# Sixteen more tokens taken out of the dense expert projection of a hybrid block, and the last gate unit in two halves

## The chip, the cores and the metric

One Trainium2 chip, one NeuronCore of it. The metric is the device time of one execution in microseconds; of the kernel before there are three runs. All data is float32; the matmuls of the large projections are float32 products made of three fp32r matmuls.

## What is computed

One layer of a trunk over 512 tokens of width 1024: a parallel mix of windowed attention and retention, then a product-key expert mixer (PEER), a gated per-layer embedding, and a final norm. The part that is changed is the expert mixer, and at the end the gate:

```python
q = (h @ w_query).reshape(B, S, PEER_HEADS, 2, half)
s1, s2 = scores of q[..., 0, :] and q[..., 1, :] with 128 sub keys each
v1, i1 = top_k(s1, 16);  v2, i2 = top_k(s2, 16)
top_s, top_pos = top_k(v1[:, None] + v2[None, :], 16)      # 16 of 256 pairs, for each of 8 heads
expert_idx = i1 * 128 + i2 of these pairs;  gates = softmax(top_s)
u = expert_down[expert_idx]                                # 128 rows of 1024 for each token
act = gelu(einsum('td,ted->te', h, u))
y = einsum('te,ted->td', act * gates, expert_up[expert_idx])
x = x + y
x = x + sigmoid(rms_norm(x) @ w_ple_gate) * (p @ w_ple_proj)
return rms_norm(x)
```

There are 128 x 128 = 16384 experts, each one row of `expert_down` and one of `expert_up`.

## The kernel before

**Stages.** Activations are kept transposed, model width on the partitions and tokens on the columns. Every weight comes as a unit of 128 x 1024 (0.5 MB); `UNITS` (line 44 on) lists all 390 in the order of their use. SP loads a unit into one of 4 `raw` slots (line 437) as soon as `lo_done` says that POOL has finished with that slot. ScalarE writes its upper part `w_hi` (line 496), POOL its lower part `w_lo` (line 450), into rings of 8, and PE multiplies in three matmuls (`mm3`, lines 848 to 850).

The expert mixer handles 384 of the 512 tokens densely, and the last 128 sparsely. For the 384 dense tokens PE computes the inner products with all 16384 rows of `peer_down`: 128 units (`down`, line 1061), each 24 matmuls of 384 columns, 8 units to a turn, 16 turns. ScalarE takes the GELU of each result (line 701) and writes pairs of units to memory (line 704). In turns 9 to 14 PE also makes the gates of all experts of a token from one-hot vectors: DVE compares the keys with an iota (`compare`, line 1531) and multiplies one of the two one-hots with the gate (`times_gate`, line 1538), for four tokens at a time, 16 such quads `q` in a turn `j`; PE multiplies them (`scatter`, line 1081) and ScalarE stages the result and writes it out (lines 707 to 719). DVE's `compare` may be four quads ahead of PE. Before that, PE transposes the selected keys and gates, after `SELECT_AT` = 3 units of turn 8 (lines 1102 to 1110). In the up projection (`up`, line 1121) DVE multiplies activations by gates (`weigh`, line 1578), ScalarE and DVE split the result (lines 771, 1595), and PE multiplies it with the 128 units of `peer_up`, 18 matmuls of 512 columns each. `weigh` reads gates and activations back from memory, in pieces issued by ScalarE (`read_back`, line 725).

**The sparse tokens** have one token on each partition. For each of 128 rows (8 heads x 16), POOL fetches 128 rows of `peer_down` by an indirect DMA into one of four slots (`u_ring`, line 470), and DVE multiplies them with the tokens' activations `h_tok` and adds up (`dot`, line 1196). `h_tok` is made once, by 16 matmuls (line 1050). Later the rows of `peer_up` are fetched and added likewise (`axpy`, line 1567).

**What sets the order.** There is no scheduler: each engine's program is written out by hand, with waits on semaphores. POOL's queue holds the lower parts unit by unit; at which unit a fetch stands in it is given by `EARLY_FETCH` and `fetch_down_at` (lines 151 to 161), for dots that DVE makes between the steps of its top-k (`together`, `best`, `decode`; 66 of them), 4 behind the exponential's argument, 6 behind the gates (`DOTS_EXP`, `DOTS_SELECT`), and then between one-hots (`DOT_QUADS`, line 1149). A fetch also waits for the dot that used its slot four rows before (line 469). ScalarE gives the upper part of unit e + 5 just before the GELU of unit e (`gelu`, line 688). At the end of the last down turn (lines 784 to 796) it also splits the first two experts' weights, and it reads back the first two pieces after the third unit.

**The end.** For each of 8 units of the gate (`pg`, line 1164) PE makes 24 matmuls of 512 columns; DVE scales, ScalarE takes the sigmoid, DVE multiplies and adds, ScalarE squares; `add_up(3)` sums the squares over partitions, and the final norm follows (lines 1625 to 1639).

## Time and profile before

| | us |
|---|---|
| three runs | 2020.37, 2021.49, 2022.61; median 2021.49 |
| profiled execution, its own time | 2022.7 |
| its span in the trace | 2020.9 |
| PE busy | 1994.2 (99%) |
| PE weight loads busy | 1760.5 (87%) |
| DVE busy | 1372.2 (68%) |
| ScalarE busy | 803.7 (40%) |
| POOL busy | 1197.5 (59%) |
| mean DMA rate | 225 GB/s |

Busy times are sums over instructions of one execution; the engines work side by side, so they do not add up to the span. Matmuls overlap, and their ends are modelled: what one costs is read from the distance between the starts, not from its duration. "Released by" names the instruction that ended a wait last.

### The profile page before, as it was taken

How to read it: one execution, taken by the hardware profiler on the slowest of the kernel's cores; microseconds unless marked ns; L12 is line 12 of the kernel's file. 1: busy time of each engine (PE TensorE's matmuls, PEld its weight loads, DVE VectorE, ACT ScalarE, POOL GpSimd, SP SyncE). 2: the span in 40 equal slices, each digit the busy share in tenths (PEclk: the TensorE clock that was granted, in tenths of full speed). 3: DMA queues.
4: the chain of work that ended last, by engine and by line, in shares of the span. 5: the costliest groups of instructions: out<-in, count | busy, mean ns of one | idle time of the engine just before them, and what ended most of it. 6: DMA issues, size and time to landing. Idle time of an engine off the chain costs nothing.

```text
span 2020.9 us, 28806 instructions
## 1 busy us (share of the span) xinstructions
PE 1994.2 (99%) x10155; PEld 1760.5 (87%) x10155; DVE 1372.2 (68%) x2241; ACT 803.7 (40%) x1075; POOL 1197.5 (59%) x650
## 2 busy tenths in 40 slices
PE   7999999999999999999999999999999999999997
PEld 6888888887888888999999999999888888888886
DVE  6424242333722399899997878782797899888946
ACT  5222222233643343333334666665443333333352
POOL 5342424243245244878888555555899888888821
PEclk9999999999999999999999999999999999999998
DMA  6232323133233322889999788888999999999911
GB/s 215 73 114 61 117 62 108 66 120 94 74 94 105 114 84 86 307 294 318 324 319 323 288 302 298 301 303 296 341 384 382 372 364 353 359 369 367 349 62 42
DMA packets 167334, 455.00 MB, mean 225 GB/s; under 512 B 13264, under 2 KB 62416, under 8 KB 165456
## 3 DMA queue, kind: packets, MB, share of 16 engines
q1 hardware_dynamic: 58032, 209.04, 30.8%
q0 software_dynamic: 36864, 134.23, 17.3%
q10 hardware_dynamic: 72352, 110.64, 16.0%
q8 instruction: 47, 0.77, 0.2%
q14 instruction: 39, 0.32, 0.0%
HBM read 396.71 MB, written 54.53 MB: 223 GB/s over the span
## 4 chain that ended last, share of the span: by engine, by line
PE 95%; DVE 2%; ACT 1%; DMA 1%; ACTq 0%; issue 0%; SPq 0%; DVEq 0%
PE bank L848 29%; PE bank L850 29%; PE bank L849 29%; PE bank L1089 4%; PE bank L955 1%; PE bank L1038 1%; PE bank L1023 1%; PE bank L999 0%; PE bank L1009 0%; DVE bank L1244 0%; DMA xT<-x_cols 0%; ACTq L731 0%; PE bank L924 0%; DVE h_lo L1252 0%; PE bank L912 0%
## 5 line engine op out<-in xcount | busy, mean ns | idle before, releaser
L450 POOL TENSOR_TENSOR w_lo<-raw,w_hi 128x1024 fp32r<-128x1024 f32 x390 | 937.6, 2412 | 709.7 <-ACT w_hi L496 706.3
L848 PE MATMUL bank<-h_hi,w_hi 128*128 128x384 f32 (+1 forms) x1552 | 560.0, 361 | 0.4 <-ACT scr L701 0.4
L850 PE MATMUL bank<-h_hi,w_lo 128*128 128x384 f32 (+1 forms) x1552 | 548.5, 353 | 0.0
L849 PE MATMUL bank<-h_lo,w_hi 128*128 128x384 f32 (+1 forms) x1552 | 548.3, 353 | 0.0
L496 ACT ACTIVATE w_hi<-raw 128x1024 fp32r<-128x1024 f32 x390 | 407.5, 1057 | 172.5 <-PE bank L850 62.6
L850 PEld LDWEIGHTS bank<-h_hi,w_lo 128*128 128x128 f32 x1552 | 291.9, 188 | 21.2
L848 PEld LDWEIGHTS bank<-h_hi,w_hi 128*128 128x128 f32 x1552 | 292.2, 188 | 20.6 <-issue 0.6
L849 PEld LDWEIGHTS bank<-h_lo,w_hi 128*128 128x128 f32 x1552 | 292.2, 188 | 20.1
L850 PE MATMUL bank<-w_hi,b_lo 128*128 128x512 f32 x768 | 298.8, 389 | 0.0
L849 PE MATMUL bank<-w_lo,b_hi 128*128 128x512 f32 x768 | 298.8, 389 | 0.0
L848 PE MATMUL bank<-w_hi,b_hi 128*128 128x512 f32 x768 | 298.8, 389 | 0.0
L1595 DVE TENSOR_TENSOR b_lo<-scr,b_hi 128x384 fp32r<-128x384 f32 x128 | 210.3, 1643 | 71.9 <-ACT b_hi L771 71.9
L1204 DVE SCALAR_TENSOR_TENSOR xT<-xT,bank 128x1024 f32<-128x1024 f32 x128 | 154.9, 1212 | 28.5 <-DMA xT<-peer_down,scr 27.9
L850 PEld LDWEIGHTS bank<-w_hi,b_lo 128*128 128x128 f32 x768 | 144.1, 188 | 30.0
L849 PEld LDWEIGHTS bank<-w_lo,b_hi 128*128 128x128 f32 x768 | 144.1, 188 | 29.9
L848 PEld LDWEIGHTS bank<-w_hi,b_hi 128*128 128x128 f32 x768 | 144.1, 188 | 29.9
L771 ACT ACTIVATE b_hi<-scr 128x384 fp32r<-128x384 f32 x128 | 67.2, 525 | 255.5 <-PE bank L850 129.2
L480 POOL DMA_INDIRECT scr<-peer_up,scr x128 | 137.6, 1075 | 51.6 <-DVE bank L1575 31.7
L1575 DVE SCALAR_TENSOR_TENSOR bank<-scr,bank 128x1024 f32<-128x1024 f32 x127 | 162.2, 1277 | 0.8
L713 ACT ACTIVATE scr<-bank 128x512 f32<-128x512 f32 x96 | 109.3, 1138 | 107.3 <-PE bank L1089 107.3
L470 POOL DMA_INDIRECT xT<-peer_down,scr x128 | 122.1, 954 | 31.0 <-issue 16.5
L701 ACT ACTIVATE scr<-bank 128x384 f32<-128x384 f32 x128 | 62.9, 492 | 176.7 <-PE bank L850 173.0
(185 smaller groups left out, 2545.0 us busy)
## 6 DMA issues: line engine op xcount, KB each, us to landing
raw<-weights SPq DMA_DIRECT2D x390, 512.0 KB, 4.6
act_scratch<-scr ACTq DMA_DIRECT2D x64, 384.0 KB, 4.8
gate_scratch<-scr ACTq DMA_DIRECT2D x12, 2048.0 KB, 8.0
scr<-gate_scratch ACTq DMA_DIRECT2D x22, 768.0 KB, 7.7
scr<-act_scratch ACTq DMA_DIRECT2D x22, 768.0 KB, 12.6
xT<-gate_scratch ACTq DMA_DIRECT2D x10, 768.0 KB, 7.5
xT<-act_scratch ACTq DMA_DIRECT2D x10, 768.0 KB, 12.1
scr<-scr ACTq DMA_DIRECT2D x20, 128.0 KB, 2.7
```

Of the source, the lines that this page charges most:

```text
L450: return nc.gpsimd.tensor_tensor(w_lo[:, s, :], raw[:, s % RAW, :], w_hi[:, s, :].bitcast(F32), ALU.subtract)
L470: pool.indirect_dma_start(u_ring[:, n % U_SLOTS, :], None, down_d, bass.IndirectOffsetOnAxis(ap=expert_of[:, n:n + 1], axis=0)).then_inc(u ...
L480: pool.indirect_dma_start(v_slot(n), None, up_d, bass.IndirectOffsetOnAxis(ap=expert_of[:, n:n + 1], axis=0)).then_inc(v_landed[n % V_SLOT ...
L496: nc.scalar.activation(w_hi[:, u_mod, :], raw[:, s, :], ACT.Copy).then_inc(hi_done, 1)
L713: nc.scalar.activation(stage[:, b, :, t:t + 4].rearrange("p j t -> p t j"), scattered(q), ACT.Copy).then_inc(stage_ready, 1)
L848: nc.tensor.matmul(out, a_hi, c_hi, start=first, stop=False)
L849: nc.tensor.matmul(out, a_hi, c_lo, start=False, stop=False)
L850: return nc.tensor.matmul(out, a_lo, c_hi, start=False, stop=last)
L1089: ins = nc.tensor.matmul(scattered(q)[:, x, :], onehot(q, x, 0).bitcast(F32), gated[q % 4][:, x, :], start=True, stop=True)
L1204: stt(out=row, in0=row, scalar=1.0, in1=h_tok, op0=ALU.mult, op1=ALU.mult, accum_out=dots[:, n:n + 1]).then_inc(dot_done, 1)
L1575: ins = stt(out=y_sparse, in0=v_slot(n), scalar=a, in1=y_sparse, op0=ALU.mult, op1=ALU.add)
L1595: tt(b_lo[:, c % 4, 0:TD], wgt[:, c % 2, :], b_hi[:, c % 4, 0:TD].bitcast(F32), ALU.subtract).then_inc(wgt_split, 1)
```

## The change

`TZ` = 368 instead of 384 tokens go through the dense down projection; the 16 tokens 368 to 383 (`NX`) take its result from fetched rows. For them the partitions are laid out as 8 groups of 16 tokens: `copies_hi` and `copies_lo` hold each token's activations 8 times (written by ScalarE), so that one fetch brings the rows of one of the 16 picks for all 8 heads of all 16 tokens, and 16 fetches bring them all. The expert numbers are computed from the transposed keys and turned onto the partitions by DVE (`turn`), and the 16 results are turned back, go through the GELU, and are multiplied into the transposed gates of these tokens; the activations in memory are 1.0 there (a memset). `h_tok` is rewritten for the copies (`REP_AT`) and again for the sparse tokens (`TOK_AT`). There are thus 144 fetches and dots instead of 128.

The order is rewritten with it: the exponential is taken after 3 units of turn 8 (`EXP_AT`) instead of at its start, the selection after 6 instead of 3. DVE makes 74 dots ahead of the one-hots instead of 76, 6 in a row behind the third quad, 10 in each of the last three scatter turns instead of 8, and the last 15 (`NLAST`) behind the last one-hot, ahead of `weigh`. All 144 fetches have units of their own in POOL's queue (`FETCH_AT`), the last at the unit 130 from the first down unit, that is the third of `peer_up`. The scatter turns 0 to 2 are written out instead of looped.

The last gate unit is made in two halves of 256 tokens, in two banks, and everything behind it up to the squares' sum as well.

```diff
+HALVES = (slice(0, S // 2), slice(S // 2, S))
 TD = S - P
 TDT = TD // P
+NX = 16
+TZ = TD - NX
 TG = 32
...
-SELECT_AT = 3
+EXP_AT, SELECT_AT = 3, 6
...
-DOTS_EXP, DOTS_SELECT, DOTS_START = 4, 6, 4
+DOTS_EXP, DOTS_SELECT = 4, 4
 DOTS_EARLY = (PH - 1) * DOTS_DECODE + (PH - PLAIN_HEADS) * DOTS_HEAD + DOTS_EXP + DOTS_SELECT
-DOT_QUADS = tuple(range(1, TG // 2, 2))
+ODD = tuple(range(1, TG // 2, 2))
+DOT_QUADS = ((2, 2, 2, 2, 2, 2, 7, 9, 11, 13, 15), ODD, (1, 3, 5, 11, 13, 15)) + 3 * (tuple(sorted(ODD + (4, 10))),)
+NMAIN = DOTS_EARLY + DOT_QUADS[0].count(2)
+NROWS = NPAIR + NX
+REP_AT, TOK_AT = (0, 1), (2, 4)
+NGATE = sum(map(len, DOT_QUADS))
+NLAST = NROWS - DOTS_EARLY - NGATE
 AXPY_LAG = 8
-EARLY_FETCH = (8, 8, 9, 9, 11, 11, 13, 14, 14, 15, 15, 16, 17, 17, 20, 21, 21, 22, 23, 24, 25, 27, 28, 29, 30, 30,
-               31, 31, 32, 33, 33, 36, 36, 37, 37, 38, 40, 40, 42, 43, 45, 45, 46, 46, 47, 47, 49, 49, 51, 51, 52,
-               52, 53, 55, 55, 57, 57, 58, 58, 59, 60, 60, 61, 63, 63, 64, 65, 65, 67, 67, 69, 69, 70, 70, 71, 72,
-               72, 73, 73, 74, 74, 75, 76, 77)
-
-
-def fetch_down_at(n):
-
-    if n < len(EARLY_FETCH):
-        return DN0 + EARLY_FETCH[n]
-    return DN0 + STEP * FIRST_Z + 10 + n - DOTS_EARLY - DOTS_START
+EARLY_FETCH = (8, 8, 9, 9, 11, 11, 14, 15, 15, 16, 16, 17, 18, 18, 21, 22, 22, 23, 24, 25, 26, 28, 29, 30, 31,
+               31, 32, 32, 33, 34, 34, 37, 37, 38, 38, 40, 42, 42, 44, 45, 47, 47, 48, 48, 49, 49, 51, 51, 53, 53,
+               54, 54, 55, 57, 57, 59, 59, 60, 60, 61, 62, 62, 63, 66, 66, 67, 68, 68, 70, 70, 72, 72, 73, 73)
+FETCH_AT = EARLY_FETCH + (74, 74, 75, 75, 76, 76)
+FETCH_AT += tuple(STEP * (FIRST_Z + 1 + j) + q // 2 + 3 for j in range(len(DOT_QUADS)) for q in DOT_QUADS[j])[6:]
+FETCH_AT += tuple(NKEY - STEP + 3 + 8 * i // NLAST for i in range(NLAST))
+assert len(EARLY_FETCH) == DOTS_EARLY and len(FETCH_AT) == NROWS
+assert all(x <= y for x, y in zip(FETCH_AT, FETCH_AT[1:])) and FETCH_AT[-1] < NKEY + LEAD
...
 FETCH_DOWN, FETCH_UP, ADD_UP_AT = {}, {}, {}
+for _s, _u in enumerate(FETCH_AT):
+    FETCH_DOWN.setdefault(DN0 + _u, []).append(_s)
 for _n in range(NPAIR):
-    FETCH_DOWN.setdefault(fetch_down_at(_n), []).append(_n)
...
+        def last_gate(x):
+
+            return bank[:, 5 - 3 * x, HALVES[x]]
...
+                for r in FETCH_DOWN.get(u, ()):
+                    extra, n = row_of(r)
+                    if r == 0:
...
+                    if extra:
+                        pool.wait_ge(extra_ready, 1)
+                    elif n % TOPK == 0:
                         pool.wait_ge(expert_ready, n // TOPK + 1)
...
-                nc.scalar.activation(act[:, c % 4, :], bank[:, c % 2, 0:TD], ACT.Gelu_apprx_tanh).then_inc(act_ready, 1)
+                nc.scalar.activation(act[:, c % 4, 0:TZ], bank[:, c % 2, 0:TZ], ACT.Gelu_apprx_tanh).then_inc(act_ready, 1)
...
-                if c == 0:
+                if c < 2:
+                    copies, h = ((copies_hi, h_hi), (copies_lo, h_lo))[c]
+                    nc.scalar.activation(copies.rearrange("p k (g t) -> p k g t", t=NX),
+                                         h[:, :, TZ:TD].unsqueeze(2).to_broadcast([P, KT, P // NX, NX]),
+                                         ACT.Copy).then_inc(copies_ready, 1)
+                if c == EXP_AT:
                     sc.wait_ge(top_ready, 1)
                     nc.scalar.activation(gate_s.rearrange("p t n -> p (t n)"), gate_s.rearrange("p t n -> p (t n)"),
                                          ACT.Exp).then_inc(gexp_ready, 1)
@@ -755,7 +792,11 @@
                 gelu(FIRST_Z, c)
...
+            for j in range(1, TOK_AT[0] + 1):
+                gate_turn(j)
+            sc.wait_ge(extra_dotted, 1)
+            nc.scalar.activation(act_extra, dots_extra, ACT.Gelu_apprx_tanh).then_inc(extra_gelu, 1)
+            with sc.Fori(TOK_AT[0] + 1, NTG // 2) as j:
                 gate_turn(j)
...
-            sc.wait_ge(dot_done, NPAIR)
+            sc.wait_ge(dot_done, NROWS)
...
-                    pe.wait_ge(sq_ready, KT * (r + 1))
                     for t in range(TT):
+                        if t % 2 == 0:
+                            pe.wait_ge(sq_ready, KT * (r + 1) + t // 2)
                         ins = nc.tensor.matmul(bank[:, 7, t:t + 1], sq[:, (KT - 1) % 2, P * t:P * t + P],
                                                ones[:, 0:1], start=False, stop=t == TT - 1)
...
+            def token_rows(of):
+
+                for k in range(KT):
+                    for n, h in enumerate((h_hi, h_lo)):
+                        ins = nc.tensor.matmul(h_tok[:, P * k:P * k + P], of(h, k), ident_r[:, :],
+                                               start=n == 0, stop=n == 1)
+                ins.then_inc(htok_done, 1)
...
-                    ins = mm3(bank[:, c % 2, 0:TD], w_hi[:, s, P * k:P * k + P], w_lo[:, s, P * k:P * k + P],
-                              h_hi[:, k, 0:TD], h_lo[:, k, 0:TD], k == 0, k == KT - 1)
+                    ins = mm3(bank[:, c % 2, 0:TZ], w_hi[:, s, P * k:P * k + P], w_lo[:, s, P * k:P * k + P],
+                              h_hi[:, k, 0:TZ], h_lo[:, k, 0:TZ], k == 0, k == KT - 1)
...
                 for c in range(STEP):
                     down(j + (FIRST_Z + 1), c, halfway=lambda: scatter(j, 2 * c))
                     scatter(j, 2 * c + 1)
+                    if isinstance(j, int) and (j, c) == REP_AT:
+                        pe.wait_ge(dot_done, NMAIN)
+                        pe.wait_ge(copies_ready, 2)
+                        token_rows(lambda h, k: (copies_hi if h is h_hi else copies_lo)[:, k, :])
+                    if isinstance(j, int) and (j, c) == TOK_AT:
+                        pe.wait_ge(dot_done, NMAIN + NX)
+                        token_rows(lambda h, k: h[:, k, TD:S])
...
-            scatter_turn(0)
-            with pe.Fori(1, NTG // 2) as j:
+            for j in range(TOK_AT[0] + 1):
+                scatter_turn(j)
+            with pe.Fori(TOK_AT[0] + 1, NTG // 2) as j:
                 scatter_turn(j)
...
+            last = UNIT[("pg", KT - 1)]
+            pe.wait_ge(lo_done, last + 1)
+            for x in range(2):
+                pe.wait_ge(pg_free, KT - 4 + x)
+                for k in range(KT):
+                    ins = mm3(last_gate(x), w_hi[:, last % RING, P * k:P * k + P], w_lo[:, last % RING, P * k:P * k + P],
+                              h_hi[:, k, HALVES[x]], h_lo[:, k, HALVES[x]], k == 0, k == KT - 1)
+                ins.then_inc(proj_done, 1)
             add_up(3)
...
+            nc.vector.memset(act[:, :, TZ:TD], 1.0).then_inc(filled, 1)
...
+            step(stt(out=ids_extra, in0=keysT[:, 0, TZ:TD], scalar=float(NKEY), in1=keysT[:, 1, TZ:TD],
+                     op0=ALU.mult, op1=ALU.add))
+            turn(ids_extra)
+            mark(tt(expert_extra, turned[:, 0, :], turned[:, 1, :], ALU.add), extra_ready)
...
                     times_gate(j, q)
-                    if j == 0 and q == 2:
-                        next_dots(DOTS_START)
-                    if q in DOT_QUADS:
-                        dot()
-
+                    next_dots(DOT_QUADS[j].count(q))
+                    if done[0] == NMAIN + NX and not extras[0]:
+                        extras[0] = 1
+                        ve.wait_ge(dot_done, NMAIN + NX)
+                        turn(dots_extra)
+                        mark(tt(dots_extra, turned[:, 0, :], turned[:, 1, :], ALU.add), extra_dotted)
+
+            extras = [0]
             compare(0, 0)
             for j in range(NTG // 2):
+                if j == NTG // 2 - 2:
+                    ve.wait_ge(extra_gelu, 1)
+                    step(tt(bank[:, 6, TZ:TD], bank[:, 6, TZ:TD], act_extra, ALU.mult))
                 one_hots(j)
             ve.wait_ge(oh_used, TD // 4)
             for k in range(2):
                 ve.wait_ge(p_hi_ready, k + 1)
                 mark(tt(b_lo[:, 4 + k, :], pT[:, k, :], b_hi[:, 6 + k, :].bitcast(F32), ALU.subtract), p_split)
+            next_dots(NLAST)
...
+            m = KT - 1
+            z = tile2[:, tiles[0] % 2, :]
+            ve.wait_ge(pproj_ready, KT)
+            for x, a in enumerate(HALVES):
+                ve.wait_ge(proj_done, OUT[("pg", m)] + 1 + x)
+                mark(tt(z[:, a], last_gate(x), rrms[:, a], ALU.mult), scaled_ready)
+                if x == 0:
+                    add_square(3, m - 1)
+                ve.wait_ge(tile_ready, tiles[0] + 1 + x)
+                step(tt(prod[:, a], z[:, a], pproj[m][:, a], ALU.mult))
+                mark(tt(xT[:, m, a], xT[:, m, a], prod[:, a], ALU.add), x_ready)
```

## Rows read from the trace of the kernel before

**Rows 1.** The page, part 4: the chain that ended last, its shares by engine.
```profile
PE 95%; DVE 2%; ACT 1%; DMA 1%; ACTq 0%; issue 0%; SPq 0%; DVEq 0%
```

**Rows 2.** Windows: stretch, length, busy PE, PEld, DVE, ACT, POOL, clock, DMA share, GB/s.
```profile
800.00:1066.00 266.00, 266.00 (x1537) 266.00 (x1536) 248.18 (x619) 98.12 (x130) 221.11 (x135) 1.00 0.88 305
...
1100.00:1388.00 288.00, 288.00 (x1933) 288.00 (x1932) 226.94 (x289) 174.54 (x193) 165.59 (x98) 1.00 0.80 294
1388.00:1420.00 32.00, 31.64 (x183) 31.35 (x183) 4.83 (x7) 13.35 (x19) 17.11 (x9) 1.00 0.96 328
```

**Rows 3.** Timeline of PE, three widths: first, last of 59, 36, 37 steps.
```profile
899.70 0.33 PE L848 MATMUL bank<-h_hi,w_hi 128*128 128x384 f32 x1
...
909.93 0.33 PE L850 MATMUL bank<-h_hi,w_lo 128*128 128x384 f32 x1
...
1995.73 0.39 PE L850 MATMUL bank<-h_hi,w_lo 128*128 128x512 f32 x1
...
2003.89 0.39 PE L850 MATMUL bank<-h_hi,w_lo 128*128 128x512 f32 x1
...
404.77 0.28 PE L848 MATMUL bank<-w_hi,h_hi 128*128 128x256 f32 x1
...
409.21 0.28 PE L849 MATMUL bank<-w_lo,h_hi 128*128 128x256 f32 x1
```

**Rows 4.** The chain in order of time: the token rows; columns start, us, what.
```profile
726.16 1.73 PE bank L1052 x16
```

**Rows 5.** Timeline of DVE from the gates to the 80th dot.
```profile
1078.26 0.23 DVE L1520 COPY scr<-scr 128x128 f32<-128x128 f32 x1
...
1085.61 1.22 DVE L1204 SCALAR_TENSOR_TENSOR xT<-xT,bank 128x1024 f32<-128x1024 f32 x1
...
1093.99 2.35 DVE L1535 TENSOR_TENSOR b_hi<-bank,scr 128x1024 fp32r<-128x1024 f32 x2
...
1096.85 1.22 DVE L1535 TENSOR_TENSOR b_lo<-bank,scr 128x1024 fp32r<-128x1024 f32 x1
...
1106.15 1.22 DVE L1204 SCALAR_TENSOR_TENSOR xT<-xT,bank 128x1024 f32<-128x1024 f32 x1 [1.19 <-DMA xT<-peer_down,scr]
```

**Rows 6.** Timeline of PE: last selection transposes, first scatter.
```profile
1079.45 0.27 PE L1109 MATMUL bank<-small,scr 128*128 128x128 f32 x1
...
1102.44 1.05 PE L1089 MATMUL bank<-scr,b_hi 128*128 128x128 f32 x8
```

**Rows 7.** Timeline of POOL: lowered weights and fetches in its queue.
```profile
1088.62 2.40 POOL L450 TENSOR_TENSOR w_lo<-raw,w_hi 128x1024 fp32r<-128x1024 f32 x1
...
1093.40 2.41 POOL L450 TENSOR_TENSOR w_lo<-raw,w_hi 128x1024 fp32r<-128x1024 f32 x1
...
1100.59 0.94 POOL L470 DMA_INDIRECT xT<-peer_down,scr  x1 [3.66 <-DVE xT L1204]
```

**Rows 8.** The fetches of peer_down rows, from issue to landing.
```profile
DMA to landing us min/median/max: 4.6/6.3/10.6
```

**Rows 9.** Timelines of POOL and of ACT in the last down turn.
```profile
1390.65 4.75 POOL L450 TENSOR_TENSOR w_lo<-raw,w_hi 128x1024 fp32r<-128x1024 f32 x2 [2.56 <-ACT w_hi L496]
...
1400.99 5.08 ACTq L731 DMA_DIRECT2D scr<-act_scratch  x1
1406.19 1.06 ACT L496 ACTIVATE w_hi<-raw 128x1024 fp32r<-128x1024 f32 x1 [6.57 <-issue]
```

**Rows 10.** The chain around the start of the up projection.
```profile
1420.49 0.23 PE bank L848
```

**Rows 11.** Windows: a pause of PE, the up stage; columns as in rows 2.
```profile
495.00:505.00 10.00, 7.98 (x33) 6.09 (x32) 9.19 (x15) 4.41 (x16) 2.34 (x1) 0.83 0.27 80
...
1430.00:1445.00 15.00, 15.00 (x68) 12.43 (x67) 13.78 (x9) 4.72 (x6) 14.28 (x9) 1.00 1.02 372
```

**Rows 12.** The chain behind the last unit.
```profile
2005.90 0.70 DVE scr L1634
...
2008.02 1.88 PE bank L904 x8
```

More of the change, by code:

```diff
@@ L212, in block_program @@
         sub_keys = small[:, 424:680].rearrange("p (a k) -> p a k", a=2)
+        same_half = small[:, 680:712].rearrange("p (a k) -> p a k", a=2)
         misc = sb("misc", [P, 128])
@@ L460, in _ @@
                 lower(u % RING).then_inc(lo_done, 1)
-                for n in FETCH_DOWN.get(u, ()):
-                    if n == 0:
+                for r in FETCH_DOWN.get(u, ()):
+                    extra, n = row_of(r)
+                    if r == 0:
                         pool.wait_ge(x_spilled, 16)
@@ L709, in stage_gates @@
                 b, t = q // (TG // 4), 4 * (q % (TG // 4))
-                if t == 0 and not isinstance(j, int):
+                if t == 0 and not (isinstance(j, int) and j == 0):
                     sc.wait_ge(gate_written[b], 16 * j)
@@ L737, in gate_turn @@
                     stage_gates(j, 2 * c + 1)
-                    if c == 1 and not isinstance(j, int):
+                    if c == 1 and not (isinstance(j, int) and j == 0):
                         store_gates(j - 1, 1)
@@ L757, in _ @@
             sc.dma_start(pT[:, :, :], pT_d).then_inc(p_landed, 16)
-            with sc.Fori(1, NTG // 2) as j:
+            for j in range(1, TOK_AT[0] + 1):
[3 more added lines that the diff above has]
+            with sc.Fori(TOK_AT[0] + 1, NTG // 2) as j:
                 gate_turn(j)
@@ L833, in _ @@
             root(2)
-            for m in range(KT):
+            for m in range(KT - 1):
                 run_ahead(UNIT[("pg", m)] + 4)
@@ L1049, in _ @@
                     pe.wait_ge(ident_ready, 1)
-                    for k in range(KT):
-                        for n, h in enumerate((h_hi, h_lo)):
-                            ins = nc.tensor.matmul(h_tok[:, P * k:P * k + P], h[:, k, TD:S], ident_r[:, :],
-                                                   start=n == 0, stop=n == 1)
-                    ins.then_inc(htok_done, 1)
+                    token_rows(lambda h, k: h[:, k, TD:S])
                 if m == 0:
@@ L1163, in _ @@
                 embed(m)
-            for m in range(KT):
+            for m in range(KT - 1):
                 columns(("pg", m), h_hi, h_lo, tiles=(u_ready, 2 * KT) if m == 0 else None,
@@ L1168, in _ @@
                     spread(2)
+            last = UNIT[("pg", KT - 1)]
+            pe.wait_ge(lo_done, last + 1)
+            for x in range(2):
+                pe.wait_ge(pg_free, KT - 4 + x)
[3 more added lines that the diff above has]
+                ins.then_inc(proj_done, 1)
             add_up(3)
@@ L1196, in dot, with turn @@
             def dot():
-                n = done[0]
+                r = done[0]
                 done[0] += 1
-                if n == 0:
-                    ve.wait_ge(htok_done, 1)
-                ve.wait_ge(u_landed[n % U_SLOTS], 16 * (n // U_SLOTS + 1))
-                row = u_ring[:, n % U_SLOTS, :]
+                extra, n = row_of(r)
+                if r in (0, NMAIN, NMAIN + NX):
+                    ve.wait_ge(htok_done, 1 + (r >= NMAIN) + (r >= NMAIN + NX))
+                ve.wait_ge(u_landed[r % U_SLOTS], 16 * (r // U_SLOTS + 1))
+                row = u_ring[:, r % U_SLOTS, :]
+                to = dots_extra if extra else dots
                 stt(out=row, in0=row, scalar=1.0, in1=h_tok, op0=ALU.mult, op1=ALU.mult,
-                    accum_out=dots[:, n:n + 1]).then_inc(dot_done, 1)
+                    accum_out=to[:, n:n + 1]).then_inc(dot_done, 1)
+            def turn(src):
+                step(tt(two_halves, src.unsqueeze(1).to_broadcast([P, 2, NX]), same_half, ALU.mult))
+                step(nc.vector.transpose(turned.rearrange("p a k -> p (a k)"), two_halves.rearrange("p a k -> p (a k)")))
             def together(instructions, more=False):
@@ L1624, in _ @@
             norm_scale(2)
-            for m in range(KT):
+            for m in range(KT - 1):
                 key = ("pg", m)
```

37 lines of the change are left out of this document (29 added, 8 removed).

## The prediction

> **What bounds the kernel now.** I read the chain of waits first: 95% of it is TensorE [rows 1]. The windows by stage say the same: from 800 to 1388 us, in which the dense down projection runs, TensorE is busy in every microsecond, and the granted clock is 1.00 [rows 2]. Only in the last down turn (1388 to 1420 us, eight groups) does it lose 0.36 us, and there the DMA engines are busy for 0.96 of the time although nothing is fetched for the sparse tokens. So a column that leaves the down matmuls is time gained, as long as nobody who feeds TensorE was just in time. The same table warns of this: DVE is busy for 248 of 266 us up to 1066. What it does there does not get shorter by the change.
>
> **Narrower matmuls.** The starts of matmuls of one width give their cost: 59 steps of 384 columns in 10.23 us are 173.4 ns, 36 steps of 512 in 8.16 us are 226.7 ns, 37 steps of 256 in 4.44 us are 120.0 ns [rows 3]. Both differences give 0.417 ns a column. 16 columns less are 6.67 ns, and there are 128 x 24 = 3072 such matmuls: **-20.5 us**. One group of 24 goes from 4.16 to 4.00 us.
>
> The Trainium skill (TensorE: Matmul & The Clock Gate, Back-to-back issue gap) speaks against this: in a stream of weight load and matmul it gives some 81 ns for 128 columns and 131 ns for 512, as an estimate 0.13 ns a column, by which the gain would be 6.4 us. The rows disagree; the measured slope is three times that.
>
> **Work added to TensorE.** The token rows are formed three times instead of once. Once is 16 matmuls in 1.73 us [rows 4], all on the path, so **+3.5 us**. The selection transposes and the one-hot products stay as they are.
>
> **First handover: top-k and one-hots to the scatter.** TensorE now reaches the same point earlier: it begins the down groups at 799.8, so the 71st begins at 799.8 + 70 x 4.00 = 1079.8, where it now makes the selection transposes (they ended at 1079.7 before, after 67 groups). The gates are ready at 1078.3 as before [rows 5], since DVE's work up to there is the same and its fetches are moved to about the same times. So the selection itself waits for nothing. But then only two and a half groups lie before the first scatter instead of five and a half: it is asked for at 1079.8 + 1.2 (nine transposes) + 8.0 + 2.0 = 1091.0, where before it was 1102.4 [rows 6]. DVE: the 74th dot ended at 1086.8 and is fetched at the same time now; with two dots less behind it, but the ids of the extra tokens (four small steps, some 1.7 us together, an estimate by the 0.23 us copy at 1078.26 with as much again for the wait behind each), the first compare is at about 1088.8 against 1093.99. Two compares and one product (1093.99 to 1096.85, 1.14 + 1.14 + 0.6) put the first one-hot at 1091.7: 0.7 us late.
>
> Three one-hots later DVE takes six dots in a row (one and four before), from 1095.1. POOL can issue the last two of these fetches only when the first two dots have freed their slots, at 1096.4 and 1097.7. In the trace the same wait is to be seen: a fetch held up until 1100.6 whose dot came at 1106.15 [rows 5, 7]. With the median 6.3 us from issue to landing [rows 8] the sixth dot ends at 1105.3, and the fourth one-hot is there at 1107.1. TensorE asks for it after 0.7 us of waiting and three steps of 2.9 us (half a group, and 0.9 for a scatter's eight matmuls, whose row shows 1.05 with the last one's end) at 1100.5: 6.3 us late. Together **+7 us**. Bounds: 2 us, if the fetches land after the 4.6 us minimum and the small steps cost nothing, and 11, with the 10.6 us maximum.
>
> From there on DVE has room: 16 x (1.14 + 0.6) + 10 x 1.23 = 40 us of work for a turn of 46.4. The other queues: the two copies of ScalarE, at some 1.06 us each, lie in its 2 us waits for TensorE; if those were gone they would delay the weights by 2 us, with five groups in hand. The memset and the second half of the gates' waits cost nothing beside them. The wait of ScalarE for the extra dots lies after a turn in which they are long done, and the wait of TensorE for the 96th dot comes four one-hots after it. SP's queue only gets its waits answered earlier.
>
> **Second handover: the last dots to the up projection.** Fifteen dots now follow the last one-hot, and DVE weighs the first experts only after them. Their fetches lie in POOL's queue, two behind each lowered weight, over units 123 to 130. A unit with two fetches takes POOL 4.78 us (1088.62 to 1093.40) [rows 7], a group takes TensorE 4.00. POOL begins unit 125 at 1390.7 [rows 9] and would be at 128 at 1405.0, but ScalarE is held for 5.08 us in issuing the read-back of the activations and gives the upper part of that unit at 1406.19 to 1407.25 [rows 9]. That it is held is due to what is in flight, so it is taken as it was. From 1407.3: two units with two fetches (9.6), one lowering (2.4) and the issue, so the last fetch goes out at 1419.5. Landing 6.3, dot 1.3, weighing, its upper and its lower part 2.2: the first expert's weights are ready at 1429.3. Before, TensorE began with them at 1420.49 without a wait [rows 10]. It would now begin at 1420.5 - 8 x 0.16 = 1419.2. So **+10.1 us**. Bounds: 5, with fast landings and the read-back issued without being held, and 19 (the third rival). Behind DVE's dots stand the weighing, then ScalarE's weight upper parts, the last GELU and the next weights' upper parts, which have five units in hand.
>
> **The clock.** Both stalls are longer than any idle time of TensorE in this stage, so it may fall from 2.4 to 1.2 GHz. Where TensorE paused for 2 us near 500 us the mean clock of 10 us was 0.83, 1.7 us of full clock lost [rows 11]. Between nothing and that for each stall I take 1.2 twice: **+2.4 us**.
>
> **The last unit in halves.** 48 matmuls of 256 columns are 5.76 us against 24 x 0.2267 = 5.44: +0.3. Behind them five elementwise steps have half their width: of 0.70 us for 512 columns [rows 12] at most half can go, and each keeps a start of its own, so I take 0.26, -1.3 us in all. Of the eight closing matmuls (1.88 us) [rows 12] half can go ahead: -0.9. **-1.8 us**, between 0 and -2.5.
>
> Sum: -20.5 + 3.5 + 7.0 + 10.1 + 2.4 - 1.8 = +0.7 us. The profiled execution took 2022.7 us, 1.8 more than its span and 1.2 more than the median; set against the median of 2021.5 the forecast is **2022.2 us**, no change that a measurement could tell (0.2%, 4 us).
>
> **Rivals.**
> *The covers hold.* Were neither handover late, 7.0 + 10.1 + 2.4 = 19.5 us go from the forecast and 2002.7 is left. If one of them holds, it is 2011 to 2014. For it: both terms hang on landings, and the spread of these (4.6 to 10.6 us) [rows 8] is as long as the lateness. Against it: three groups of slack are taken from the first handover, and POOL's 37 us (8 x 2.4 + 15 x 1.2) of lowering and fetching in a last turn of 32 us, make TensorE late without any late landing. 0.14 for both, 0.20 for one.
> *No time per column here.* Between 128 columns (1.73 us / 16 = 108 ns) and 256 (120 ns) the spacing hardly follows the width; were this so at 368, the gain would be 3072 x 1.5 ns = 4.5 us. TensorE would come 2.3 us early to the first handover, which had 2.5 in hand, and the second would cost 9: -4.5 + 3.5 + 9 + 1.2 - 1.8 = +7.4, 2029 us. It decides if the next spacing is over 171 ns. Against it: two equal slopes in rows 3. 0.03.
> *The last down turn becomes bound by transfers: slower.* 1388 to 1420 moved 328 GB/s x 32 us = 10.5 MB. 13 fetches of 0.52 MB come on top: 17.3 MB, at the 372 GB/s of 1430 to 1445 [rows 11] 46.5 us. The last fetch lands at 1434.5 and TensorE begins at 1438: 8.7 us more, 2031 us. It decides as soon as the last landing takes more than some 10 us, or the read-back is held for over 9. For it: that stretch's share of 0.96 [rows 2] without any fetch. Against it: the weights run several units ahead, and a busy share does not say that no more could be moved. 0.21. The Trainium skill (Perfetto Trace Analysis, Roofline) puts a single core's ceiling at some 435 GB/s; by that estimate the stretch would take 39.8 us, and no stage of this trace holds such a rate.
>
> **How the numbers follow.** Forecast, both handovers late as worked out: 0.42; its own range is 2017 to 2028 by the bounds of both. Faster by over 4 us: the first rival's 0.34, and 0.03 from the lower end of the forecast. Slower by over 4 us: 0.03 + 0.21 + 0.04 from its upper end, 0.28. Same: 0.35. The range leaves out the full success and the worst of the transfers: 2008 to 2032.
>
> **What would show it.** The down matmuls at 166.7 ns; TensorE waiting 5 to 8 us for DVE at its fourth scatter near 1100 us, the dot before it waiting for a DMA; at the start of the up projection 8 to 12 us of waiting for DVE's lower part, with the last dot of L1204's line just ahead and POOL without a gap; granted clock below 1 behind both; the last PE pieces followed by shorter DVE pieces. The forecast is wrong if TensorE's busy time over its span stays at 99% and the down stage is 17 us shorter, or if ScalarE's issue of the first read-back holds TensorE much longer than the 0.36 us of now.

## The result: 2059.5 us, 1.9% slower

The changed kernel took 2059.5 us (median of four runs, 2052.6 to 2069.7), the kernel before beside it 2020.9 (2020.3 to 2022.6): ratio 1.019, 95% interval 1.017 to 1.022. The forecast was 2022.2, the range 2008 to 2032. The runs of the changed kernel also differ by 17 us, those of the kernel before by 2. The profiled execution has a span of 2061.7 us, 40.8 more than before; all lines below are from profiled executions, one of each kernel.

**The profile after.** The chain that ended last, by engine, and from part 5 of the page the groups of the dot products and of their fetches (busy, mean ns, idle before and what ended it):

```profile
PE 72%; DVE 12%; DMA 7%; POOL 4%; issue 3%; ACT 2%; ACTq 1%; DVEq 0%; SPq 0%; POOLq 0%
...
L1276 DVE SCALAR_TENSOR_TENSOR xT<-xT,bank 128x1024 f32<-128x1024 f32 x144 | 174.2, 1213 | 117.4 <-DMA xT<-peer_down,scr 114.2
...
L501 POOL DMA_INDIRECT xT<-peer_down,scr x144 | 137.1, 952 | 68.7 <-DVE xT L1276 42.6
```

TensorE's share of the chain fell from 95% [rows 1] to 72%. VectorE now waits 114 us for expert rows; before it was 28. The windows, with the columns of [rows 2], show where TensorE stands:

```profile
1050.00:1100.00 50.00, 42.21 (x243) 41.64 (x241) 41.80 (x76) 20.23 (x27) 37.71 (x25) 0.90 0.86 290
1100.00:1150.00 50.00, 38.50 (x228) 38.17 (x228) 38.01 (x50) 18.17 (x21) 20.93 (x13) 0.83 0.49 160
...
1122.00:1132.00 10.00, 9.84 (x42) 9.84 (x43) 5.29 (x7) 1.08 (x1) 0.00 (x0) 0.52 0.30 106
...
1165.00:1415.00 250.00, 241.10 (x1641) 238.39 (x1640) 192.85 (x256) 147.42 (x167) 142.01 (x89) 0.99 0.82 301
...
1400.00:1450.00 50.00, 39.82 (x236) 39.54 (x235) 20.00 (x32) 18.26 (x24) 31.92 (x24) 0.90 1.04 387
```

There are two places with idle TensorE and a granted clock below 1 (1050 to 1150, 1400 to 1470), and a thin loss of 8.9 us in 250 between them. TensorE's timeline has 13 gaps over 0.25 us in this stage, 44.9 us together. These are the first matmuls behind six of them (start, length, line, and in brackets the idle time and its releaser):

```profile
1082.72 0.65 PE L897 MATMUL bank<-h_hi,w_hi 128*128 128x368 f32 x1 [7.79 <-ACT scr L732]
...
1107.54 1.86 PE L1143 MATMUL bank<-scr,b_hi 128*128 128x128 f32 x7 [7.51 <-DVE scr L1625]
...
1122.16 2.07 PE L1143 MATMUL bank<-scr,b_lo 128*128 128x128 f32 x8 [3.98 <-DVE scr L1625]
...
1167.45 0.82 PE L1143 MATMUL bank<-scr,b_hi 128*128 128x128 f32 x5 [1.19 <-DVE scr L1625]
...
1440.55 0.65 PE L897 MATMUL bank<-h_hi,w_hi 128*128 128x368 f32 x1 [10.18 <-ACT scr L732]
...
1461.62 0.77 PE L897 MATMUL bank<-w_hi,b_hi 128*128 128x512 f32 x1 [6.49 <-DVE b_lo L1684]
```

The 7.79 us: the gelu that should have freed a bank stands on ScalarE behind the exponentials, and these wait for VectorE's search. Then come the first scatter, the fourth, the first and the ninth scatter of the turns `j` = 1, 3, 4 and 5, that is the head of each half turn (eight gaps between 0.27 and 2.10, as the one shown; 8.9 in all), a gelu behind the read-back in the last down turn, and the start of the up projection.

**Where VectorE is late.** In the search (800 to 1080 us) the same small steps take longer than before. First the changed kernel, then the kernel before; columns: busy us, mean ns:

```profile
L1577 DVE TENSOR_TENSOR scr<-scr 128x256 f32<-128x256 f32 x16 | 20.0, 1307 | 0.6
...
L1563 DVE SCALAR_TENSOR_TENSOR scr<-scr 128x16 uint32<-128x16 f32 x8 | 17.8, 2219 | 0.3
...
L1556 DVE CAST scr<-scr 128x128 f32<-128x128 uint32 x8 | 3.9, 486 | 0.3
```
```profile
L1499 DVE TENSOR_TENSOR scr<-scr 128x256 f32<-128x256 f32 x16 | 16.7, 1103 | 0.6
...
L1485 DVE SCALAR_TENSOR_TENSOR scr<-scr 128x16 uint32<-128x16 f32 x8 | 14.0, 1746 | 0.3
...
L1478 DVE CAST scr<-scr 128x128 f32<-128x128 uint32 x8 | 1.8, 227 | 0.3
```

A step on 16 elements takes 2.2 us on average, and 0.17 at the least. The timelines of VectorE and of GpSimd (POOL) in the changed kernel say why. Three pairs, each a VectorE row and then the GpSimd row beside it; the first row merges three candidate additions, of 0.41, 7.98 and 0.41 us:

```profile
1044.89 8.65 DVE L1577 TENSOR_TENSOR scr<-scr 128x256 f32<-128x256 f32 x3
...
1045.80 7.12 POOL L477 TENSOR_TENSOR w_lo<-raw,w_hi 128x1024 fp32r<-128x1024 f32 x3
...
955.96 3.79 DVE L1563 SCALAR_TENSOR_TENSOR scr<-scr 128x16 uint32<-128x16 f32 x1
...
954.95 4.75 POOL L477 TENSOR_TENSOR w_lo<-raw,w_hi 128x1024 fp32r<-128x1024 f32 x2
...
1101.48 3.02 DVE L1605 TENSOR_TENSOR scr<-scr 128x16 uint32<-128x16 f32 x1
...
1102.12 2.35 POOL L477 TENSOR_TENSOR w_lo<-raw,w_hi 128x1024 fp32r<-128x1024 f32 x1
```

The small step of the other two pairs ends 0.05 and 0.03 us after the lowering (GpSimd's instruction that makes `w_lo`) does, once after two lowerings in a row (954.95 + 4.75 = 959.70 against 959.75). Of the eight steps of line 1563 the six long ones all end 0.04 to 0.05 us after a lowering; the two of 0.17 us met none. The addition of 7.98 us ended 0.29 us behind the third lowering in a row (another one took 5.64, over two). The Trainium skill (SBUF — State Buffer, Who interferes with whom) states the rule: a VectorE instruction with two inputs in SBUF contends with a GpSimd instruction that reads SBUF, over a port pair that is an exclusive lock. The trace agrees for these steps, and shows besides that one of them can wait for two or three GpSimd instructions and not only for one. The two shifts, which have one input, are held too (up to 3.00 us; 0.18 to 0.20 otherwise). This contention is called the port below. How long such a step takes thus hangs on its phase against GpSimd's lowerings, and the change gave these a new pace (4.00 us a unit for 4.16).

### The profile page after: what moved, and what is told of

Same layout as the page of the kernel before. It is cut to its first block, busy times and chain, and to the rows that moved or that the text cites. A ratio compares the mean times of both kernels' runs of the same rounds, so it can differ in the third digit from the quotient of the medians.

```text
span 2061.7 us, 28872 instructions
## 1 busy us (share of the span) xinstructions
PE 1991.5 (97%) x10211; PEld 1755.1 (85%) x10211; DVE 1395.9 (68%) x2285; ACT 803.8 (39%) x1080; POOL 1211.4 (59%) x666
## 4 chain that ended last, share of the span: by engine, by line
PE 72%; DVE 12%; DMA 7%; POOL 4%; issue 3%; ACT 2%; ACTq 1%; DVEq 0%; SPq 0%; POOLq 0%
PE bank L897 22%; PE bank L899 22%; PE bank L898 22%; DMA xT<-peer_down,scr 6%; POOL w_lo L477 3%; DVE xT L1276 3%; PE bank L1143 2%; POOL xT L501 1%; DVE scr L1577 1%; DVE scr L1563 1%; PE bank L1005 1%; PE bank L1088 1%; ACT w_hi L527 1%; DVE scr L1557 1%; DVE scr L1562 1%
## 5 line engine op out<-in xcount | busy, mean ns | idle before, releaser
L897 PE MATMUL bank<-h_hi,w_hi 128*128 128x368 f32 (+2 forms) x1560 | 558.1, 358 | 18.0 <-ACT scr L732 18.0
L899 PE MATMUL bank<-h_hi,w_lo 128*128 128x368 f32 (+2 forms) x1560 | 547.0, 351 | 0.0
L898 PE MATMUL bank<-h_lo,w_hi 128*128 128x368 f32 (+2 forms) x1560 | 546.9, 351 | 0.0
L1276 DVE SCALAR_TENSOR_TENSOR xT<-xT,bank 128x1024 f32<-128x1024 f32 x144 | 174.2, 1213 | 117.4 <-DMA xT<-peer_down,scr 114.2
L501 POOL DMA_INDIRECT xT<-peer_down,scr x144 | 137.1, 952 | 68.7 <-DVE xT L1276 42.6
L732 ACT ACTIVATE scr<-bank 128x368 f32<-128x368 f32 x128 | 61.0, 477 | 148.6 <-PE bank L899 134.8
```

What stands on the lines that cost most here:

```text
L501: pool.indirect_dma_start(u_ring[:, r % U_SLOTS, :], None, down_d, bass.IndirectOffsetOnAxis(ap=ids[:, n:n + 1], axis=0)).then_inc(u_lande ...
L897: nc.tensor.matmul(out, a_hi, c_hi, start=first, stop=False)
L898: nc.tensor.matmul(out, a_hi, c_lo, start=False, stop=False)
L899: return nc.tensor.matmul(out, a_lo, c_hi, start=False, stop=last)
L1276: stt(out=row, in0=row, scalar=1.0, in1=h_tok, op0=ALU.mult, op1=ALU.mult, accum_out=to[:, n:n + 1]).then_inc(dot_done, 1)
```

## The experiments

**The small steps' operands in PSUM, changed kernel (e1) and kernel before (e2).** Lines of the changed kernel:

```diff
-ts(posu[:, :, 0, :], pos[:, :, h, :], 4, None, ALU.logical_shift_right)
+ts(posu_p[:, :, 0, :], pos[:, :, h, :], 4, None, ALU.logical_shift_right)
 ...
+step(nc.vector.tensor_copy(sel1_p, sel[:, TDT, 1, :]))
-mark(stt(out=expert_of[:, at], in0=sel[:, TDT, 0, :], scalar=float(NKEY), in1=sel[:, TDT, 1, :],
+mark(stt(out=expert_of[:, at], in0=sel[:, TDT, 0, :], scalar=float(NKEY), in1=sel1_p,
 ...
+step(nc.vector.tensor_copy(val_p, val[:, :, m - 1, :]))
-val[:, t, m - 1, :].unsqueeze(2).to_broadcast([P, TOPK, TOPK])
+val_p[:, t, :].unsqueeze(2).to_broadcast([P, TOPK, TOPK])
```

> The changed kernel with VectorE's small two-operand steps of the expert search given one operand (or their result) in PSUM: the candidate additions (16 of them), the joining of the two halves of an expert's number (8) and the two shifts (16); three short copies into PSUM are added per head. What is computed stays the same. Port theory (these steps stand still while GpSimd's 2.4 us lowering reads the on-chip memory, and that is why the search ended 10.4 us late): the candidate addition falls from 1.31 to about 0.35 us and the joining from 2.22 to about 0.2 us, the subtraction ahead of the exponentials ends at 1062 or earlier instead of 1079.2, the gap of 7.8 us at the exponentials and that of 7.5 us at the first scatter go, and the time is about 2044 (2038 to 2050). Fetch theory (the search was late because each dot product waited for its expert row): those steps stay as long as they were, or the search ends within 2 us of 1079, and the time is 2059 give or take 6.

> The same edit of VectorE's small steps on the kernel before, as a control. Port theory: the steps become shorter by the same amounts and the search ends 10 us or more earlier than 1068.8, but TensorE hardly waited for it there, so the time is 2021 give or take 4. Fetch theory: nothing moves, 2021. Over 5 us faster would mean that TensorE was held by the search in the kernel before too.

e1: 2049.2 us (2048.5 to 2050.4), 10.3 less than the changed kernel, and the spread fell from 17 to 2 us. The steps, by form:

```profile
L1582 DVE TENSOR_TENSOR scr<-bank,scr 128x256 f32<-128x256 f32 x16 | 5.7, 418 | 0.1
...
L1567 DVE SCALAR_TENSOR_TENSOR scr<-scr,bank 128x16 uint32<-128x16 f32 x8 | 1.4, 172 | 0.3
```

Every one of the eight joinings now takes 170 to 174 ns. The search (up to the subtraction ahead of the exponentials) ends at 1067.1 instead of 1079.2. It had been expected at 1062: the additions, joinings, shifts and casts became 41.6 us shorter together, but between 800 and 1080 VectorE now waits 47.7 us for rows instead of 18.4, since these are fetched by a plan made for a slower VectorE. The gap at the exponentials is gone, that at the first scatter is 1.3 for 7.5. What stayed are the fourth scatter (5.4), the heads of the half turns (10.9) and the last turn (17.2); so 2049 came and not 2044. e2: 2022.4 against 2022.0, interval 0.999 to 1.001; its search ends at 1063.7 instead of 1068.8 (10 us or more had been expected, 5.1 came), and TensorE waited for it in neither. So the port decides only where the change had used up the slack.

**The down projection at 368 tokens alone, without and with the PSUM operands (e3, e9).**

```diff
-ins = mm3(bank[:, c % 2, 0:TD], ..., h_hi[:, k, 0:TD], h_lo[:, k, 0:TD], ...)
+ins = mm3(bank[:, c % 2, 0:TZ], ..., h_hi[:, k, 0:TZ], h_lo[:, k, 0:TZ], ...)
```

> The kernel before with the down projection and its gelu at 368 tokens instead of 384 and nothing else: the fetches, the dot products, the stage plan and the tail are those of the kernel before. It leaves out the down projection of 16 tokens (a 1 stands in for their activations). Term theory (3072 matmuls, 6.67 ns each, covered): 2000.5. Port theory: TensorE reaches the exponentials some 6 us earlier while VectorE's search ends where it was or later, so TensorE waits there, and the time is about 2006 to 2012, with the subtraction ahead of the exponentials at 1066 to 1079. Fetch theory: VectorE is as early as in the kernel before or earlier, and the time is 2000 to 2002.

> e3_narrow (the kernel before with the down projection at 368 tokens and nothing else) with the small steps' operands in PSUM as in e1_ports. It leaves out the down projection of 16 tokens, as e3_narrow does. Port theory (the 9 us by which the narrower matmuls gave less than 20.5 in e3_narrow are VectorE's search, late by its waits for GpSimd's lowering): the subtraction ahead of the exponentials ends at 1060 or earlier instead of 1064.5, the gap of 5.7 us at the exponentials goes, and the time is 2003 (2001 to 2005). Rival (the transfers, whose rows are fetched by the unit and so come at a faster pace too): the gap stays above 3 us and the time at 2007 or more.

e3: 2010.4 us (2008.3 to 2019.4), 11.6 less than before where the columns alone are worth 20.5. TensorE stood here:

```profile
1068.08 0.64 PE L853 MATMUL bank<-h_hi,w_hi 128*128 128x368 f32 x1 [5.70 <-ACT scr L705]
```

e9: 2002.7 us (2000.5 to 2004.8), 19.4 less than before, and that gap is gone; one of 1.7 us is left at a scatter. The search ends at 1064.5 in e3 and at 1057.8 in e9. For e3 the port theory had the time and the gap right and the end of the search wrong: it is 4.3 us earlier than before, not later, while the exponentials are asked for 12 us earlier. With only the width changed, no token moved and the schedule of before, the port takes 7.8 us of the gain, and the spread falls with it from 11 us (six runs) to 4 (four). This is the plainest of the comparisons.

**The last 15 rows left out (e4).**

```diff
-NLAST = NROWS - DOTS_EARLY - NGATE
+NLAST = 0
+NROWS = DOTS_EARLY + NGATE
-FETCH_AT += tuple(NKEY - STEP + 3 + 8 * i // NLAST for i in range(NLAST))
```

> The changed kernel without the 15 expert rows and dot products of the last down turn (neither fetched nor multiplied; their activations are left out of the sum, the additions of the up rows stay). Last-turn theory (the dots behind the last scatter cost 6.5 us, and their fetches beside the gates' store and the read-back hold ScalarE's queue for 10.2 us of TensorE): both gaps go, the hold falls from 8.7 to about 5 us, and the time is about 2042. Rival (the hold comes from the store and the read-back alone): only the gap of 6.5 goes, the hold stays at 8 us or more, and the time is about 2052.

2040.0 us (2036.7 to 2046.2), 19.5 less than the changed kernel. Issues of the read-back in ScalarE's queue, first in the changed kernel, then in e4 (start, how long the issue held the queue):

```profile
1422.97 6.55 ACTq L762 DMA_DIRECT2D scr<-act_scratch  x1
...
1430.14 8.73 ACTq L762 DMA_DIRECT2D scr<-act_scratch  x1
```
```profile
1420.43 0.66 ACTq L762 DMA_DIRECT2D scr<-act_scratch  x1
...
1421.70 4.80 ACTq L762 DMA_DIRECT2D scr<-act_scratch  x1
```

Before it was 5.08 [rows 9]. In all eleven traces the longer of the two holds is 8.5 to 9.2 us in the three kernels with these 15 rows (changed kernel, e1, e5) and 4.3 to 5.1 in the eight others. Without the rows the two holds fall from 15.3 to 5.5 us, the gap of 10.2 to 0.35, and that of 6.5 us goes. Both came from the 15 rows: the last-turn theory holds, its rival falls. The sum of both is 16.7 us. Behind them the granted clock was 0.72 and 0.74 over 10 us each in the changed kernel, which is 5.4 us lost; that the rest of the 19.5 is less than this is within the spread of the runs.

**Rows of the scatter turns fetched one unit earlier (e5, on top of e1).**

```diff
-FETCH_AT += tuple(STEP * (FIRST_Z + 1 + j) + q // 2 + 3 for j in ...)[6:]
+FETCH_AT += tuple(STEP * (FIRST_Z + 1 + j) + q // 2 + 2 for j in ...)[6:]
```

> The kernel of e1_ports with each expert row of the scatter turns fetched one weight unit (5.8 us) earlier, the order unchanged. Fetch theory for the turns (at each turn's second quad VectorE waits 4 to 7 us for a row whose landing is slowed to some 10 us by the gates' store, and passes 1.2 to 1.9 us of it to TensorE's first scatter of the turn): the ten small gaps at the turns' first scatters go (12.3 us in all, without those of the first turn 10.9), and the time is about 2038 (2036 to 2041). Rival (VectorE has too much work in a turn, so that it is late whatever the rows do): the gaps stay, 2049.

2035.0 us (2034.7 to 2037.5), 14.2 less than e1, 1 us under the expected range. The expectation has the place of the wait wrong: it is behind a turn's eighth and its last quad, not at its second. Windows of e1 and of e5, same columns:

```profile
1150.00:1400.00 250.00, 238.93 (x1636) 235.95 (x1635) 192.08 (x256) 146.80 (x166) 141.19 (x89) 1.00 0.81 299
```
```profile
1150.00:1400.00 250.00, 250.00 (x1718) 250.00 (x1718) 195.06 (x255) 149.85 (x169) 149.05 (x94) 1.00 0.87 319
```

All 11 us at the heads of the half turns went, by a fetch moved, with VectorE as busy as before: the forecast had counted VectorE's work (40 of 46.4 us) and not when the rows of a turn arrive. The other 3 us of the 14.2 are not assigned.

**A layout for all four, with and without the PSUM operands (e6, e7).** On top of e1; beside these lines the first 86 fetches have new units, those of the turns stand one unit earlier, and the numbers of the extra experts are worked out behind the second quad:

```diff
-REP_AT, TOK_AT = (0, 1), (2, 4)
+REP_AT, TOK_AT = (0, 2), (2, 2)
-DOT_QUADS = ((2, 2, 2, 2, 2, 2, 7, 9, 11, 13, 15), ODD, (1, 3, 5, 11, 13, 15)) + 3 * (...)
+DOT_QUADS = ((2, 2, 3, 3, 4, 5, 9, 11, 13, 15), tuple(sorted(ODD + (4, 10))), (1, 3, 9, 10, 11, 13, 14, 15)) + 3 * (
+    (0, 1, 3, 4, 5, 7, 8, 9, 11, 12, 13, 15),)
-step(nc.vector.tensor_reduce(sel.rearrange("p t a k -> p (t a) k"), p4, AX_X, ALU.add))
+together([lambda: nc.vector.tensor_reduce(sel.rearrange("p t a k -> p (t a) k"), p4, AX_X, ALU.add)], h >= 2)
```

> The kernel of e1_ports with its dot products laid out anew: 6 more in the expert search (a third one in each decoding of a head from the third on), 12 instead of 10 in each of the last three scatter turns, none in the last down turn; the early rows are fetched as soon as a slot of the ring is free; the six behind the third quad are spread over quads 2 to 5; the two handovers of the token rows stand two quads ahead of the first dot that needs them; the numbers of the 16 extra experts are worked out behind the second quad. All four of the gap theories together (port, last turn, turn starts, first handover): of the 35 us of gaps in e1_ports under 6 are left, and the time is 2012 to 2018, below the kernel before. Rival (the transfers are full: the engines' share of 0.96 in the search leaves no room for 6 more rows, and the rows become late again): gaps of 10 us or more before the first scatter or in the last turns, 2025 to 2035.

> The kernel of e6_spread with VectorE's small two-operand steps back in the on-chip memory as in the changed kernel. Port theory: these steps cost some 30 us more in the search again, the subtraction ahead of the exponentials ends at about 1080, and TensorE waits 8 us at the exponentials and some at the first scatter: about 2028 (2022 to 2035), with a spread of the runs of 5 us or more against 2 to 3 us. Fetch theory (the search is bound by the rows, which now come as early as a slot is free): within 3 us of e6_spread.

e6: **2003.0 us** (2002.5 to 2004.3), ratio to the kernel before 0.990 (0.989 to 0.992), 56.5 us below the changed kernel and below the range expected. The page's chain and the windows of three stretches:

```profile
PE 95%; DVE 3%; ACT 1%; DMA 1%; issue 0%; DVEq 0%; SPq 0%; ACTq 0%
```
```profile
1080.00:1130.00 50.00, 50.00 (x344) 50.00 (x342) 44.49 (x56) 27.48 (x33) 31.42 (x19) 1.00 0.76 263
1300.00:1350.00 50.00, 50.00 (x348) 50.00 (x347) 43.42 (x59) 31.27 (x35) 33.39 (x22) 1.00 0.97 354
1350.00:1403.00 53.00, 53.00 (x340) 52.80 (x339) 20.11 (x30) 27.68 (x35) 29.14 (x15) 1.00 0.93 331
```

One gap of 0.26 us is left of the 44.9, and the clock stays at 1.00. The transfers' share is 0.97 in the second of them, with twelve rows a turn, and TensorE waits for nothing, so the transfers were not the bound (the rival falls). The pieces of this layout were not run one by one, so which of them freed the fourth scatter is not shown. e7: 2009.9 us (2006.4 to 2011.5), 6.9 more than e6. Its search ends at 1065.7 against 1049.4 in e6, six gaps of 0.4 to 1.3 us are back, and the spread is 5 us against 1.8. Neither theory named this (about 2028, or within 3 us of e6): the steps did cost 23.3 us more in the search (39.5 against 16.2), but with the rows fetched as soon as a slot is free, e6 is done with the search 20 us before ScalarE begins the exponentials (1069.6), and this slack takes most of the waits in. So the port alone does not cost the 38.6 us between the two kernels, and neither does the plan of the rows; each eats what would have covered the other.

**The last unit in halves alone (e8).** The matmuls and what follows them, applied to the kernel before:

```diff
-for m in range(KT):
+for m in range(KT - 1):
 ...
+for x in range(2):
+    for k in range(KT):
+        ins = mm3(last_gate(x), ..., h_hi[:, k, HALVES[x]], h_lo[:, k, HALVES[x]], k == 0, k == KT - 1)
+    ins.then_inc(proj_done, 1)
```

> The kernel before with the last unit in halves and nothing else. Forecast term: 1.8 us shorter, 2019.4. The trace of the changed kernel, whose stretch from the last transposes to the end is 2.7 us shorter: 2018.5. Rival (the stretch got shorter through something else of the change): 2021.

2020.5 us (eleven runs, 2017.8 to 2023.1) against 2022.1, ratio 0.999 (0.998 to 1.000). Set against these 2022.1 us the forecast term gives 2020.3 and the rival 2022.1; the interval of the ratio reaches 1.000, so the reading rests on the trace. From the first matmul of the up projection to the end it is 598.8 us instead of 600.6, in e6 598.7. The steps as foreseen:

```profile
2004.88 0.58 PE L918 MATMUL bank<-small,scr 128*128 128x1 f32 x4
2006.70 1.01 PE L918 MATMUL bank<-small,scr 128*128 128x1 f32 x4 [1.24 <-ACT scr L853]
```

Half of the eight closing matmuls [rows 12] now go ahead, and 1.0 us is left behind the last square. The term of 1.8 us is right (its three parts add up to 1.9).

## Why the prediction was wrong

**Narrower matmuls, -20.5: right.** In the changed kernel 73 steps of 368 columns take 12.17 us, 166.7 ns each, as foreseen:

```profile
898.77 0.33 PE L897 MATMUL bank<-h_hi,w_hi 128*128 128x368 f32 x1
...
910.94 0.33 PE L898 MATMUL bank<-h_lo,w_hi 128*128 128x368 f32 x1
```

The slope of [rows 3] holds at this width, and the rival of no time per column is out. By this row the estimate of 0.13 ns a column, worked out from the Trainium skill (TensorE: Matmul & The Clock Gate, Back-to-back issue gap), is out too. **Token rows, +3.5: right** at full clock: in e6, where nothing stalls, down and scatter stage together are 17.2 us shorter, and -20.5 + 3.5 is -17.0. **The last unit, -1.8: right** (e8).

**The first handover, +7.0: failed in the sentence "The gates are ready at 1078.3 as before, since DVE's work up to there is the same ... So the selection itself waits for nothing".** The instructions were the same, not their time. The search ended 10.4 us later (3.3 more of waiting for rows, 9.2 more in the three forms shown above; against them it had begun 1.1 earlier and other forms fell by fractions of a microsecond), the exponentials held ScalarE's gelus, and TensorE stood for 7.8 us. The sentence before it failed with it, that the 74th dot "is fetched at the same time now": its fetch went out at 1089.4 instead of 1079.4, and in e1, where nothing stands at the exponentials, at 1080.4. So VectorE came to the last two dots of the selection before their rows (4.8 and 2.2 us of waiting), and one of the "four small steps, some 1.7 us together" took 3.0. So the first compare began at 1104.5 instead of 1088.8, the first scatter cost 7.5 us instead of 0.7 and the fourth 4.0 instead of 6.3: with the 7.8 it is 19.3 us for 7.0 (by the prediction's own times the fourth is 6.6 late, 1107.1 - 1100.5, and the term 7.3). The prediction took the 248 of 266 busy us in [rows 2] as work. They contained small steps held for up to 3.3 us. Against the means of e1 some 34 us of it were waits (11.0 in the candidate additions, 12.6 in the joinings, 10.0 in the shifts).

**"From there on DVE has room": failed, 8.9 us instead of 0.** A turn's work does fit. But in each half turn one row takes 8.8 to 10.6 us to land, with 2 MB of gates being stored, and VectorE waited 3 to 7 us for it behind the eighth and the last quad, ahead of the one-hots for the next scatter. A fetch and its dot, before and in the changed kernel:

```profile
1233.32 0.95 POOL L470 DMA_INDIRECT xT<-peer_down,scr  x1
...
1242.41 1.22 DVE L1204 SCALAR_TENSOR_TENSOR xT<-xT,bank 128x1024 f32<-128x1024 f32 x1
...
1252.13 0.95 POOL L501 DMA_INDIRECT xT<-peer_down,scr  x1
...
1262.01 1.22 DVE L1276 SCALAR_TENSOR_TENSOR xT<-xT,bank 128x1024 f32<-128x1024 f32 x1 [6.88 <-DMA xT<-peer_down,scr]
```

The row was as slow before (9.1 us here). But VectorE then came to it 9.1 us after the fetch had been issued, and now 3.0. The diff says why: `fetch_down_at` put the fetch for quad `q` of turn `j` at unit `STEP * (FIRST_Z + 1 + j) + q // 2 + 2`, the change writes `+ 3`. The prediction did not price this unit. e5 takes it back, VectorE comes 8.8 us after the fetch, and the gaps are gone.

**The second handover, +10.1: late as foreseen, but by another path for the larger part.** It was 16.7 us. Only 6.5 of it is the wait foreseen, for VectorE's lower part at the start of the up projection. The other 10.2 is TensorE waiting for a gelu that stands on ScalarE behind the read-back, which the prediction had named as a sign of being wrong. The step that failed is "That it is held is due to what is in flight, so it is taken as it was": the hold of 5.08 us became 6.55 + 8.73. The sum comes close to the third rival, which had 18.8 (10.1 + 8.7) for this handover, but neither of its two signs came: no hold was over 9 us, and the last row landed 6.4 us after its fetch, though others of the fifteen took 10 to 12.5.

**The clock, +2.4: 17.0, the largest error of all terms.** Two stalls at 1.2 us each had been taken; there were thirteen gaps, and six of them cost clock. From the first down matmul to the first of the up projection the changed kernel took 662.9 us, before 620.6, and of the difference of 42.3 us, 44.9 are gaps and -17.0 the work, so 14.4 are left for the low clock, and 2.6 more behind the last gap (0.74 over 10 us). The windows of some 10 us behind the five longest gaps of this stretch (7.8, 7.5, 4.0, 2.1 and 10.2 us) give 13.7 by themselves. The lower level is plainly seen in the window from 1122 to 1132, shown above: 0.52, 1.2 GHz nearly throughout, on top of 9.8 busy us. The sixteen matmuls of the token rows lie in it, at 213 ns a step instead of 111 in e6. Behind gaps of 1.1 to 1.3 us (in e1 up to 1.9) the windows show 1.00, behind that of 2.1 us 0.83, behind those of 4 to 10 us 0.5 to 0.83.

The terms measured, -20.5 + 3.5 + 19.3 + 8.9 + 16.7 + 17.0 - 1.8 = 43.1, stand against 42.3 - 0.5 = 41.8 us for the two stretches from the first down matmul to the end; the first began 1.1 us earlier, which gives the 40.8 within 0.1. A rest of 1.3 us is not accounted for. The chances had 0.28 on slower, and the range ended at 2032: each of the two unknown holds had been bounded, but as one lateness each, not as a chain of several in which every stop also costs clock.

The rival "the covers hold" was priced at 2002.7 us. That is what the same change gives once the covers are there (e6, 2003.0). It needs the PSUM operands for this: without them (e7) it is 2009.9.

## What to carry to other kernels

Before slack in front of a handover is spent, look at the mean and the minimum of every small instruction of the engine that delivers: a step of 16 elements with a mean of 2 us and a minimum of 0.17 is waiting inside its own record, and its length will move with another engine's phase. Put one operand of each such step in PSUM. A column removed is worth its full price only if every delivery (search, fetched rows, the queue that also issues transfers) is moved by as much; plan the fetches from the time a slot is free, not from the place of their use. And price a stall of TensorE not by its length alone: here those of 2 to 10 us cost another 1.7 to 4.8 us each at a low clock, and those of 1.1 to 1.9 us nothing that the windows show.

## What was new about the hardware

- A VectorE step with both inputs in SBUF can be held by GpSimd's 2.4 us elementwise instruction up to the end of two or three of them (3.8 to 4.1 us for 16 elements, 7.98 us at most for 256). The lowerings took no more than 2.43 us in the search and 2.91 in the whole changed kernel. With one operand in PSUM the 16-element step takes 170 to 174 ns, the 256-element one at most 425. The two shifts took up to 3.00 us with their result in SBUF and 0.22 to 0.23 with it in PSUM. Of the eight casts from SBUF to SBUF one took 2.30 us in the changed kernel, the others 226 to 228 ns; in e1, with the source in PSUM, all take 291 to 293.
- The time of the whole kernel is less certain with such waits: 17 us between four runs of the changed kernel, 11 between six of e3, against 1.8 to 4.4 between four each of e1, e5, e6 and e9. The kernel before, which has the same steps but time in hand, spread by 4.7 and 6.0 over fifteen runs each, and with the PSUM operands (e2) by 5.0 over ten.
- Issuing one read-back of 768 KB in the last down turn held ScalarE's queue for 8.5 to 9.2 us with fifteen gathers of 512 KB in the same turn, and for 4.3 to 5.1 us without them. Which resource makes the issue wait no run has separated.
- DMA engines at a share of 0.97 and 354 GB/s (e6, 1300 to 1350) left no wait on TensorE; that the share was near 1 had said little about what could still be added.
